# Context keys and router queries of an expert kernel: products and evictions planned at separate steps

## The reference

```python
for l in range(2):
    h  = modulate(x,   norm1_g[l], m_x[0], m_x[1])
    hc = modulate(ctx, norm1_g[l], m_c[0], m_c[1])
    if last:  kv_c = keys_values(hc)      # rmsnorm(hc @ w_kv) @ w_ukv, no rope
    else:     mix_c, kv_c = token_mix(hc) # attention, Fourier and pool branches
    x = x + m_x[2] * token_mix(h, kv_c)
    x = x + m_x[5] * peer(modulate(x, norm2_g[l], ...))
    if not last:
        ctx = ctx + m_c[2] * mix_c
        ctx = ctx + m_c[5] * peer(modulate(ctx, norm2_g[l], ...))

def peer(h):                              # 8 heads, 16 of 16384 experts each
    q = h @ w_pq                          # per head two halves of 128
    s = q . keys                          # 128 scores a half
    top 16 of each half -> top 16 pairs -> 128 experts a token, softmax gates
    a = sum over d of peer_down[expert] * h
    return sum over experts of gate * gelu(a) * peer_up[expert]
```

## Time and profile before

| | |
|---|---|
| median of three runs | 4160.32 us (4160.32 to 4169.17) |
| profiled execution, its own time | 4172.86 us |
| its span | 4171.6 us |
| PE busy | 3669.1 us, 88% |
| DVE busy | 2321.4 us, 56% |
| ACT busy | 657.2 us, 16% |
| POOL busy | 1283.5 us, 31% |
| HBM read | 1204.79 MB |
| mean TensorE clock granted | 0.95 |

### The profile page before, as it was taken

How to read it: one execution, slowest core, us unless ns; L and a number is a source line. 1 busy time by engine, 2 the same in 40 slices (tenths; PEclk the granted TensorE clock), 3 DMA queues, 4 the chain that set the end, 5 groups by cost and what they waited for, 6 DMA issues and landing times. The chain is left out here.

```text
span 4171.6 us, 41042 instructions
## 1 busy us (share of the span) xinstructions
PE 3669.1 (88%) x14584; PEld 2587.9 (62%) x14584; DVE 2321.4 (56%) x5464; ACT 657.2 (16%) x1800; POOL 1283.5 (31%) x1125
## 2 busy tenths in 40 slices
PE   8988999998998889999998988777878898877777
PEld 6667788887856778888746874333335786433333
DVE  3432011557767887766751156766763126777875
ACT  2332001110001320100002211111112211111111
POOL 1100000000655566665620013433441002344443
PEclk9999999999999999999999999888999999998889
DMA  8742344334998889998963359988996327999998
GB/s 319 282 194 90 123 151 182 121 129 148 410 396 306 291 327 402 405 383 351 413 250 115 106 223 357 407 344 365 416 414 269 109 106 296 380 420 420 417 419 332
DMA packets 207818, 1208.65 MB, mean 290 GB/s; under 512 B 23696, under 2 KB 24848, under 8 KB 96000
## 3 DMA queue, kind: packets, MB, share of 16 engines
q0 software_dynamic: 154368, 855.71, 51.3%
q1 hardware_dynamic: 53248, 350.32, 22.1%
HBM read 1204.79 MB, written 1.15 MB: 289 GB/s over the span
## 5 line engine op out<-in xcount | busy, mean ns | idle before, releaser
L1308 PE MATMUL bank<-big 128*128 128x256 f32 (+5 forms) x9848 | 2141.4, 378 | 59.8 <-issue 8.7
L1308 PEld LDWEIGHTS bank<-big 128*128 128x128 f32 (+2 forms) x9848 | 1833.9, 191 | 373.6 <-issue 68.0
L2499 POOL DMA_INDIRECT big<-in_pboth,big x1024 | 1219.9, 1191 | 1229.2 <-PE bank L1695 734.8
L1695 PE MATMUL bank<-big 128*128 128x512 f32 x2048 | 1006.0, 650 | 273.5 <-ACT big L2463 273.5
L2179 DVE CUSTOM_DVE_ANT_0 big<-big 128x1024 f32<-128x1024 f32 x768 | 927.5, 1224 | 322.1 <-DMA big<-in_pboth,big 305.4
L1695 PEld LDWEIGHTS bank<-big 128*128 128x128 f32 x2048 | 415.3, 208 | 855.3 <-issue 497.4
L2486 POOL TENSOR_TENSOR big<-big 128x1 f32<-128x1 f32 (+1 forms) x49 | 37.7, 769 | 1502.2 <-DVE big L1749 1502.2
L2190 DVE SCALAR_TENSOR_TENSOR big<-big 128x1024 f32<-128x1024 f32 x254 | 326.3, 1284 | 60.6 <-DMA big<-in_pboth,big 36.6
L2463 ACT ACTIVATE big<-big 128x128 f32<-128x128 f32 x512 | 164.7, 391 | 241.9 <-DVE big L2158 237.0
L1343 PE MATMUL bank<-big 128*128 128x128 f32 x596 | 95.5, 296 | 64.0 <-ACT big L2310 20.6
L2453 ACT ACTIVATE big<-big 128x4 f32<-128x4 f32 (+2 forms) x134 | 27.7, 207 | 725.2 <-DVE big L2154 718.4
(11 more groups left out here) (203 smaller groups left out, 2178.5 us busy)
## 6 DMA issues: line engine op xcount, KB each, us to landing
big<-in_w SPq DMA_DIRECT2D x104, 1024.0 KB
big<-in_wmod POOLq DMA_DIRECT2D x48, 1024.0 KB, 8.6
big<-in_wgu SPq DMA_DIRECT2D x44, 1024.0 KB
big<-in_wzg SPq DMA_DIRECT2D x36, 1024.0 KB, 4.8
big<-in_wro SPq DMA_DIRECT2D x32, 1024.0 KB
big<-in_wpq SPq DMA_DIRECT2D x24, 1024.0 KB, 7.0
big<-in_wd SPq DMA_DIRECT2D x22, 1024.0 KB
big<-in_pboth,big POOLq DMA_INDIRECT x1024, 10.1
```

Of the source, the lines that this page charges most:

```text
L1308: last = pe.matmul(o, a, b, start=(i == 0), stop=(i == n - 1))
L1695: last = pe.matmul(u.ap, d.ap, row[:, 512 * i:512 * i + 512], start=(k == 0), stop=(k == 127))
L2499: g.indirect_dma_start(out=s.ap, out_offset=None, in_=table, in_offset=bass.IndirectOffsetOnAxis(ap=index, axis=0)).then_inc(s.full[0], 16)
```

## The change

Three parts.

1. *Late queries.* Item `peer_q` keeps PE's product; the copy becomes an item of its own, `peer_q_out`, which `score(i)` puts right before `peer_scores`. This holds in all three expert stages. `peer_scores` is split in the same way, with both halves one after the other.
2. *Context keys apart.* `context_keys` calls a new `apart_keys_values`, in which each product and each eviction is an item and a yield stands between them. `modulate` does the same for its turns when it is given `room`, which only `context_keys` gives.
3. *Every twelfth step.* The side generator is advanced at step 64 and each twelfth step after.

The other users of `low_rank`, `low_turn`, `key_rope`, `kv_up` and `col_turn` put the split items one after the other, in the order that each engine had.

```diff
@@ context_keys
-        self.ctx_kv_ok = yield from self.keys_values(self.ps, Ring(self.wx), self.smallb, ar, 1, hT, hT_ok, self.KC,
-                                                     self.VC, None)
+        self.ctx_kv_ok = yield from self.apart_keys_values(self.ps, Ring(self.wx), self.smallb, ar, 1, hT, hT_ok,
+                                                           self.KC, self.VC)
@@ modulate
-            put("col_turn", h=h[:, tt, :], us=us, dst=hT[:, :, tt * P:(tt + 1) * P], done=done[tt], gain=gain, shift=shift,
-                cols_ok=self.cols_ok, r=None if vec or tt else rs[0])
-            yield 3
+            args = dict(h=h[:, tt, :], us=us, dst=hT[:, :, tt * P:(tt + 1) * P], done=done[tt], gain=gain, shift=shift,
+                        cols_ok=self.cols_ok, r=None if vec or tt else rs[0])
+            put("col_turn", **args)
+            if room:
+                yield
+            put("col_turn_out", **args)
+            if tt or not room:
+                yield 3
@@ new
+    def apart_keys_values(self, banks, wr, sm, ar, l, hT, hT_ok, K, Vv):
...
+        low = self.low_rank(banks, sm, [w], wt, hT, hT_ok, P, ckn)
+        yield
+        put("low_rank_out", **low)
+        u = banks.take()
+        w.free(u.full)
+        put("key_rope", wt=wt, hT=hT, u=u)
+        yield
+        put("low_rank_mid", **low)
+        put("key_rope_out", u=u, K=K)
+        yield
+        put("low_rank_scale", **low)
+        yield
+        turn = self.low_turn(banks, sm, P, ckn, ckvT, self.col[l, "kvg"], low["scaled"])
+        yield
+        put("low_turn_out", **turn)
+        w = self.load(wr, t["wukv"][l], 1024)
+        for at in range(0, 6, 2):
+            us = [banks.take() for _ in range(2)]
+            args = dict(w=w, ckvT=ckvT, K=K, Vv=Vv, ku=us if at < 4 else [], vu=us if at == 4 else [], at=at,
+                        ready=turn["parts"][1].free)
+            put("kv_up_made", ws=[] if at else [w], **args)
+            yield
+            put("kv_up_out", **args)
...
@@ routing
-            put("peer_q", ws=ws, w=w, u=u, hT=hT, ready=hT_ok if i == 0 else None, qt=qt)
+            put("peer_q", ws=ws, w=w, u=u, hT=hT, ready=hT_ok if i == 0 else None)
...
-            put("peer_scores", u=v, qt=qt, keys=keys, i=i, sc=sc, SC1=SC1, ready=u.free, keys_ok=keys_ok if i == 0 else None)
+            put("peer_q_out", u=u, qt=qt)
+            put("peer_scores", u=v, qt=qt, keys=keys, i=i, ready=u.free, keys_ok=keys_ok if i == 0 else None)
+            put("peer_scores_out", u=v, i=i, sc=sc, SC1=SC1)
@@ peer_x
-            if n >= 64 and n % 10 == 4:
+            if n >= 64 and n % 12 == 4:
@@ scalar_program
-    def low_rank(n, u, tmp, r, scaled, **_):
+    def low_rank_out(n, u, tmp, r, **_):
+        s.wait_ge(*u.full)
+        squares(r, halves(by2(u.ap[:, 0:2 * n])), halves(tmp))
+
+    def low_rank_scale(n, u, tmp, r, scaled, **_):
         o = by2(u.ap[:, 0:2 * n])
-        s.wait_ge(*u.full)
-        squares(r, halves(o), halves(tmp))
         s.wait_ge(*r.done)
         s.wait_ge(*r.ss)
@@ vector_program and gpsimd_program: low_rank_mid is the old low_rank
```

More of the change, by code:

```diff
@@ L784, in low_rank, with low_scaled @@
         r = self.rstd(sm, 2, 1.0 / n, EPS)
-        scaled = [self.tick("lowrank_rows"), u.free]
-        self.put("low_rank", ws=ws, wt=wt, hT=hT, ready=ready, n=n, u=u, tmp=tmp, r=r, scaled=scaled)
-        return u.full, scaled
+        args = dict(wt=wt, hT=hT, ready=ready, n=n, u=u, tmp=tmp, r=r, scaled=[self.tick("lowrank_rows"), u.free])
+        self.put("low_rank", ws=ws, **args)
+        return args
+    def low_scaled(self, args):
+        self.put("low_rank_out", **args)
+        self.put("low_rank_mid", **args)
+        self.put("low_rank_scale", **args)
     def low_turn(self, banks, sm, n, tmp, dst, gcols, scaled):
         parts = [banks.take() for _ in range(2)]
-        self.put("low_turn", n=n, tmp=tmp, dst=dst, gcols=gcols, parts=parts, scaled=scaled)
-        return parts[1].free
+        args = dict(n=n, tmp=tmp, dst=dst, gcols=gcols, parts=parts, scaled=scaled)
+        self.put("low_turn", **args)
+        return args
     def keys_values(self, banks, wr, sm, ar, l, hT, hT_ok, K, Vv, cs):
@@ L800, in keys_values @@
         wt = w.ap[:, 0:1280].rearrange("p (k n) -> p k n", k=8)
-        _, scaled = self.low_rank(banks, sm, [w], wt, hT, hT_ok, P, ckn)
+        low = self.low_rank(banks, sm, [w], wt, hT, hT_ok, P, ckn)
+        self.low_scaled(low)
         u = banks.take()
@@ L817, in keys_values @@
         w.free(vu[1].full)
-        put("kv_up", ws=[w], ckvT=ckvT, K=K, Vv=Vv, ku=ku, vu=vu, ready=turned)
+        put("kv_up", ws=[w], w=w, ckvT=ckvT, K=K, Vv=Vv, ku=ku, vu=vu, at=0, ready=turn["parts"][1].free)
         yield 6
         return [r, ku[3].free, vu[1].free]
+    def apart_keys_values(self, banks, wr, sm, ar, l, hT, hT_ok, K, Vv):
+        put, tick, t = self.put, self.tick, self.t
+        ckn = ar.get(256, (2, 128))
+        ckvT = ar.get(256, (1, 256))
+        w = self.load(wr, t["wkv"][l], 8 * 160)
+        wt = w.ap[:, 0:1280].rearrange("p (k n) -> p k n", k=8)
+        low = self.low_rank(banks, sm, [w], wt, hT, hT_ok, P, ckn)
+        yield
+        put("low_rank_out", **low)
+        u = banks.take()
+        w.free(u.full)
+        put("key_rope", wt=wt, hT=hT, u=u)
+        yield
+        put("low_rank_mid", **low)
+        put("key_rope_out", u=u, K=K)
+        yield
+        put("low_rank_scale", **low)
+        yield
+        turn = self.low_turn(banks, sm, P, ckn, ckvT, self.col[l, "kvg"], low["scaled"])
+        yield
+        put("low_turn_out", **turn)
+        w = self.load(wr, t["wukv"][l], 1024)
[6 more added lines that the diff above has]
+            put("kv_up_out", **args)
+            if at == 2:
+                k_ok = us[1].free
+        w.free(us[1].full)
+        return [u.free, k_ok, us[1].free]
     def mixer(self, banks, wr, sm, ar, l, hT, hT_ok, X, vec, rope_on, cs):
@@ L885, in mixer @@
         w = self.load(wr, t["wcq"][l], 2048)
-        made, scaled = self.low_rank(banks, sm, [w], w.ap.rearrange("p (k n) -> p k n", k=8), hT, None, 256, cqn)
-        w.free(made)
+        low = self.low_rank(banks, sm, [w], w.ap.rearrange("p (k n) -> p k n", k=8), hT, None, 256, cqn)
+        self.low_scaled(low)
+        w.free(low["u"].full)
         yield
@@ L896, in mixer @@
             kv_ok += self.ctx_kv_ok
-        turned = self.low_turn(banks, sm, 256, cqn, cqT, self.col[l, "qg"], scaled)
+        low = self.low_turn(banks, sm, 256, cqn, cqT, self.col[l, "qg"], low["scaled"])
+        put("low_turn_out", **low)
+        turned = low["parts"][1].free
         next(fill, None)
@@ L1560, in key_roped, with kv_up @@
         pe.matmul(u2.ap[0:96, 0:256], p.pmat, rt[:, 0, :], start=True, stop=True).then_inc(u2.full[0], 1)
-    def kv_up(ws, ckvT, ku, vu, ready, **_):
-        w = ws[0].dst
+    def kv_up(w, ckvT, ku, vu, at, ready, **_):
         pe.wait_ge(*ready)
-        pe.wait_ge(*ws[0].full)
+        pe.wait_ge(*w.full)
+        w = w.dst
         for j, u in enumerate(ku):
@@ L1982, in row_scale_v, with col_turn_out @@
         v.tensor_scalar(dst, src, by, None, ALU.mult).then_inc(done[0], 1)
-    def col_turn(us, dst, gain, shift, cols_ok, **_):
+    def col_turn_out(us, dst, gain, shift, cols_ok, **_):
         u = us[1]
@@ L1990, in col_turn, with low_rank_mid, low_turn_out @@
         i.then_inc(u.free[0], 1)
-    def low_rank(r, **_):
+    def low_rank_mid(r, **_):
         spread(r)
-    def low_turn(n, dst, gcols, parts, **_):
+    def low_turn_out(n, dst, gcols, parts, **_):
         for tt, u in enumerate(parts):
@@ L2382, in key_roped, with kv_up @@
         s.copy(K[64:96, :, :], bcm(rt[64:96, 0, :], 8)).then_inc(done[0], 1)
-    def kv_up(K, ku, **_):
-        for j, u in enumerate(ku):
+    def kv_up(K, ku, at, **_):
+        for j, u in enumerate(ku, at):
             s.wait_ge(*u.full)
@@ L2432, in token_gate, with peer_q_out @@
         last.then_inc(u.free[0], 1)
-    def peer_q(u, qt, **_):
+    def peer_q_out(u, qt, **_):
         if qt.before:
@@ L2502, in gpsimd_program @@
     kinds = dict(consts=consts, mod_weights=mod_weights, row_stats=root, group_stats=root, score_v=root,
-                 low_rank=root, fetch=fetch)
+                 low_rank_mid=root, fetch=fetch)
     for kind, args in p.items:
```

18 lines of the change are left out of this document (8 added, 10 removed).

## The result

The changed kernel takes 4145.86 us (median of five runs, 4140.41 to 4146.94) against 4167.24 us for the kernel before on the same chip (median of five, 4160.32 to 4169.17). The ratio is 0.9951, with a 95% interval of 0.9936 to 0.9966: 21 us less, 0.5%. The forecast was 19.2 us less. As an absolute time, 4141 us, it was 5 us too low, because it stood on the first three runs of the kernel before (4160.32) and the five have 4167.24. The profiled execution took 4146.82 us.

A forecast was written before the change was run, and what follows sets the result against it. DMA was taken to bound the expert stages, losing 30.6 us beside the context's keys, and PE the late-query places. Terms -24.6 + 7.2 - 1.8 = -19.2 us, from 4160.3 to 4141 us; range 4127 to 4158.

The forecast's parts named there:

- The keys apart: First layer's expert stage: waits between side product and eviction go, restoring DMA rate; 28.6 us gained, 4 paid, -24.6 us.
- the price of twelve pieces: First layer's expert stage, from step 88: twelve side-work calls cost 4 us, bounds 0 and 13.
- The context's routing: 740 to 900 us: five query copies move behind the other stream's eviction, delaying PE 1.45 us each; +7.2 us.
- In front of the loops: Before each of two expert loops: query 1's copy falls behind head 0's exp, delaying PE; +5.9 us a stage.
- Inside the loops: Steps 8 to 31, two stages: PE's waits of 1.03 and 3.05 us go, with 1.7 us slow clock; -6.8 us each.
- The x stages' queries together: Both expert stages with late queries: +5.9 us before each loop and -6.8 inside, -0.9 a stage; -1.8 us.
- The signs in the profile: Rate 2720 to 2870 over 405 GB/s, POOL waits over 9 us gone after step 40, five PE waits, score 1 4 us later.
- The slower one: First layer, steps 88 to 220: eight products behind fresh batches starve DMA, 41 us; 4178 us in all, chance 0.06.
- The one in which late copies bring nothing inside the loop: Expert loops: VectorE, not ScalarE, holds the next batch, so both stages pay 5.9 us in front; 4155 us, chance 0.18.
- The one in which nothing is paid: Pieces cost nothing in the first layer's stage and VectorE's ranking hides the routing's late copies; 4129 us, chance 0.16.
- The upper bound for the pieces: First layer's expert stage: every side-work piece costs its upper bound, 13 us in all; 4150 us, chance 0.09.
- POOL held back by VectorE: VectorE, no longer standing still, delays POOL's issues, some 1 us at each of ten recoveries; 4151 us, chance 0.03.

The follow-up runs named there:

- the selective form: Changed kernel, but only queries 5 to 7 of the two x stages, inside the expert loops, are late: 4122.45 us against 4165.47, ratio 0.9900.

## Why the prediction was right, term by term

- **The keys apart, forecast -24.6 us.** Right in its mechanism and some 4 us small in size. The kernel with the keys apart and no late query is 28.4 us faster. In the traces steps 84 to 144 went from 181.4 (183.9 again) to 153.7 us: -27.7 to -30.2, and the steps behind them added 0.5 to 0.8. The gross gain was set at 28.6. The step that was mis-sized is the price of twelve pieces, 4 us (upper bound 13): the traces leave at most 1.7 us for it. It had been read from two light pieces in the stretch from 2600 to 2720, whose loss was not shown to be theirs: the kernel before reads 408 and 413 GB/s there in its two executions, the changed kernel 417 and the one with no late query 411.
- **The context's routing, forecast +7.2 us.** Five waits of 1.31 us and 5.7 + 1.3 = 7.0 us in the trace; 10 us by the ratios of the runs with and without it, whose intervals (0.0015 on either side) hold both.
- **In front of the loops, forecast +5.9 us each.** Against the executions without the wait of 3.49 us (18.5 and 18.8 us) it is +6.6 to +7.0. The wait of PE came to 4.95 us as said (5). The forecast's other 1.7 us, for a slower clock behind the wait, was the author's estimate, and no run shows it there; what the trace shows in its place is 2.8 us, score 1 in 2.05 us instead of 1.13 and query 2 behind it in 8.99 us instead of 7.10, at a granted clock of 0.61 from 2480 to 2486.
- **Inside the loops, forecast -6.8 us each.** In the changed kernel -5.9 and -6.3 against the kernel with no late query (90.3 and 92.0), -9.3 and -8.2 against the kernel before, executed again (93.7 and 93.9). The kernel with the context's queries early gives only -3.5 in layer 1 (88.5 against 92.0). Both waits of 1.03 us and the one of 3.05 us went, and the waits for the scores stayed, as said.
- **The x stages' queries together, forecast -1.8 us.** Against the kernel with no late query the changed kernel pays 13.9 us in front of the loops and gets 12.2 back, +1.7; the kernel with only these queries late differs from it by -1.8 us in the medians and +1 us in the ratios. That the sum is near nothing is shown, its sign is not.
- **The signs in the profile.** The rate from 2720 to 2870 is 415 GB/s (over 405 was asked), the five waits on PE are there, score 1 starts 4.2 us later against the exp, and the part up to the context's first gather is 8 us longer, not 12. One sign failed: POOL's waits over 9 us did not all go (9.19 us at 2879). POOL's waits were a poor sign, since those of 8.94 and 6.90 us cost next to nothing; but this one stands where the rate fell to 357 GB/s.
- **The rivals.** The slower one, that each product behind a fresh batch starves DMA, is true of whole pieces (8 to 10 us over the kernel before in that stretch) and falls for the changed kernel, where twelve steps lie between. The one in which late copies bring nothing inside the loop falls with the kernel that is late only there. The one in which nothing is paid is half right: the pieces cost next to nothing, but the context's late copies were not hidden. The upper bound for the pieces, 13 us, falls with the same rows. POOL held back by VectorE is not seen either: 94.35/88 = 1.07 us an issue from 2920 to 3140, and 417 GB/s.

Against the kernel with no late query, the terms measured are -28.4 for the keys, +7.0, +13.9 and -12.2, or -19.7 us; the forecast's sum was -19.2 and the measured difference is -21. So the total is in part luck: the keys brought 3.8 us more than forecast, and the queries of the `x` stages 3.5 us less (2.1 in front of the loops, 1.4 inside them).

## What to carry to other kernels

Where several engines walk one ordered list, a side product in a stage with a full queue on TensorE should have its eviction put at least one batch's length later: here four steps, 10 us, already gave nearly all of 29 us, and smaller pieces behind fresh batches without that distance gave nothing. The same move cost 7.0 us in the context's routing and 6.9 and 7.0 us in front of the two loops, where PE was the bound and ScalarE had something slow in between (an eviction of 0.59 us in the routing, an exp that it stood 10.37 us for in front of the first loop): look, for each place, at what stands between the old and the new position on the evicting engine, and who waits for the evicted tile. Apply such a change place by place; in this kernel the selective form brought 43 us, the form applied everywhere 21. And take a term of a few microseconds from more than one execution: here the one trace that the forecast rested on held a wait of 3.49 us that the next did not have.

## What was not expected of the hardware

Two executions of the same kernel differ by 5.9 us in a single stretch (1417.5 and 1411.6 us between two fixed instructions) and in where the clock falls: from 2430 to 2600 us the record of the granted clock has stretches of 3.4 us at 0.50 of full that begin at 2483.2, 2496.9 and 2558.3 in the one and at 2439.0, 2486.8, 2548.2 and 2592.6 in the other. The part in front of the first expert product took 22.6 us in the one and 18.8 us in the other. In the six traces with the wait of PE before score 1 (4.94 to 4.96 us), in both layers' stages, the record of the clock has a stretch of 6.8 us at 0.50 around the wait's end; the seven without the wait have no stretch of that length there. In the changed kernel's first layer it begins at 2477.8, before the wait has ended at 2479.01, so the granted clock of 0.61 above (2480 to 2486) is the mean over its last 4.6 us at 0.50 and 1.4 us at 1.00.
